# Two transformer layers on one core: the first norm taken by rows of tokens as x is loaded, and the feed-forward run on unnormed activations

## What is computed

```
def rms_norm(x, w):
    y = x * rsqrt(mean(x * x, axis=-1) + EPS)
    return y * w

# first layer
h = rms_norm(x, norm1_w)
u = h @ w_in                     # split into rnn_x, rnn_gate, q, k, v, iq, ik, iw, g
...                              # recurrent branch, indexed sparse attention, gates
x = x + merged @ w_out
h2 = rms_norm(x, norm2_w)
x = x + square(relu(h2 @ w_ff_in)) @ w_ff_out      # hidden width 4096

# second layer
u = rms_norm(x, norm1_g)
...                              # differential attention, Hyena mixer
x = x + expert_choice_ffn(rms_norm(x, norm2_g), ...)   # 16 experts, 201 MB of weights
```

## Time and profile before

| | |
|---|---|
| median of 3 runs | 1281.13 us (1275.34 to 1282.58) |
| profiled execution, its own time | 1277.17 us |
| its span | 1275.4 us |
| mean granted TensorE clock | 0.968 of full |
| PE busy | 1145.8 us (90%) |
| DVE / ACT busy | 506.4 us (40%) / 400.8 us (31%) |
| transfers | 309.32 MB, mean 243 GB/s |

### The profile page before, as it was taken

How to read it: one execution, slowest core, us unless ns; L and a number is a source line. 1 busy time by engine, 2 the same in 40 slices (tenths; PEclk the granted TensorE clock), 3 DMA queues, 4 the chain that set the end, 5 groups by cost and what they waited for, 6 DMA issues and landing times.

```text
span 1275.4 us, 16258 instructions
## 1 busy us (share of the span) xinstructions
PE 1145.8 (90%) x6528; PEld 802.6 (63%) x6528; DVE 506.4 (40%) x969; ACT 400.8 (31%) x768; POOL 16.3 (1%) x28
## 2 busy tenths in 40 slices
PE   5999998999989999989899999698897888789886
PEld 4788887877889999989577888333232323233231
DVE  2356666478376755567867532300100010001001
ACT  2241555664466644466244520200000000000000
POOL 3000000000000000000000000000000000000000
PEclk9899999989989999999999999799998999999999
DMA  6153333143235666635123195399999999999997
GB/s 215 67 207 132 133 132 133 66 149 133 94 113 190 197 175 173 180 133 198 66 77 122 67 383 211 132 393 428 428 429 429 428 429 429 429 429 428 428 425 295
DMA packets 93900, 309.32 MB, mean 243 GB/s; under 512 B 5968, under 2 KB 38872, under 8 KB 81880
## 3 DMA queue, kind: packets, MB, share of 16 engines
q1 hardware_dynamic: 93256, 307.49, 62.4%
q0 software_dynamic: 496, 1.07, 0.4%
q10 hardware_dynamic: 96, 0.02, 0.0%
HBM read 307.53 MB, written 1.05 MB: 242 GB/s over the span
## 4 chain that ended last, share of the span: by engine, by line
PE 65%; DMA 26%; DVE 5%; ACT 2%; issue 1%; SPq 0%; DVEq 0%; ACTq 0%
PE bank L422 64%; DMA arena<-in_w_up 16%; DMA arena<-in_w_down 9%; DVE rstd L1501 2%; DVE parts L1535 1%; DMA cst<-table 1%; ACT parts L1169 0%; ACT root L1123 0%; PE bank L522 0%; PE bank L618 0%; SPq L1062 0%; DVE xh L1510 0%; DVE arena L1650 0%; DVE arena L1805 0%; DVE arena L1808 0%
## 5 line engine op out<-in xcount | busy, mean ns | idle before, releaser
L422 PE MATMUL bank<-parts 128*128 128x256 f32 (+1 forms) x2640 | 341.3, 291 | 8.4 <-DVE parts L1549 8.1
L422 PEld LDWEIGHTS bank<-parts 128*128 128x128 f32 x2640 | 328.7, 194 | 24.5 <-issue 20.7
L422 PE MATMUL bank<-arena 128*32 128x512 f32 (+6 forms) x724 | 267.8, 537 | 18.3 <-DVE arena L1650 5.7
L1535 DVE TENSOR_TENSOR parts<-ring,parts 128x512 fp32r<-128x512 f32 x288 | 193.1, 689 | 122.0 <-ACT parts L1169 120.7
L1169 ACT ACTIVATE parts<-ring 128x512 fp32r<-128x512 f32 x288 | 178.1, 628 | 185.7 <-PE bank L422 184.4
L422 PE MATMUL bank<-parts_room,arena 128*32 128x512 f32 x384 | 166.9, 628 | 20.5 <-DMA arena<-in_w_up 11.2
L422 PEld LDWEIGHTS bank<-arena 128*32 128x32 f32 (+3 forms) x724 | 103.8, 173 | 51.4 <-issue 35.1
L2001 DVE TENSOR_TENSOR arena<-bank,arena 128x512 f32<-128x512 f32 x8 | 5.1, 685 | 278.0 <-ACT arena L1444 278.0
L422 PE MATMUL bank<-cst,arena 128*32 128x512 f32 (+2 forms) x226 | 98.1, 589 | 17.5 <-DMA arena<-in_w_gate 8.2
L422 PE MATMUL bank<-xh,arena 128*32 128x512 f32 (+1 forms) x224 | 94.1, 596 | 16.4 <-DMA parts_room<-in_w_up 8.2
L422 PE MATMUL bank<-hidden_parts,parts 128*128 128x256 f32 x768 | 92.3, 283 | 0.0
(11 more groups left out here) (249 smaller groups left out, 828.7 us busy)
## 6 DMA issues: line engine op xcount, KB each, us to landing
ring<-in_w_in SPq DMA_DIRECT2D x22, 2048.0 KB, 7.9
ring<-in_w_gate SPq DMA_DIRECT2D x16, 2048.0 KB, 27.1
parts_room<-in_w_up SPq DMA_DIRECT2D x16, 2048.0 KB, 27.1
ring<-in_w_ff_in SPq DMA_DIRECT2D x8, 2048.0 KB, 8.6
ring<-in_w_ff_out SPq DMA_DIRECT2D x8, 2048.0 KB, 9.0
cst<-in_w_gate SPq DMA_DIRECT2D x8, 2048.0 KB, 24.0
arena<-in_w_gate SPq DMA_DIRECT2D x8, 2048.0 KB, 28.5
xh<-in_w_up SPq DMA_DIRECT2D x8, 2048.0 KB, 25.6
```

What stands on the lines that cost most here:

```text
L422: return nc.tensor.matmul(o, lhsT=l, rhs=r, start=first, stop=last)
L1535: X.tensor_tensor(w_part[1][:, p % PIECES], piece_of(n, p), w_part[0][:, p % PIECES].bitcast(F32), ALU.subtract).then_inc(S("pieces split" ...
```

## The change

At the start, the sums of squares are taken while tokens still lie over partitions: ACT squares the first 128 tokens and DVE the last 128, with a running sum, then one root and one reciprocal of 128 x 2. Each half is scaled by its row factor and PE turns the scaled rows as well (16 more transposes, into banks 0 to 3); DVE and ACT write `hT` from there, times `norm1`. `squares(0)`, `norm_stats(0)` and `norm(0, "norm1")` are gone. x is loaded in two halves, unit 0 is issued right behind them, the identity and the row of `norm1` go by ACT's queue, and the rest of the table and of the vectors follow unit 0.

In the feed-forward, ACT rounds `xT` times `norm2` into `ff_part` without the token factor, block by block as blocks become final, and DVE takes the rests. relu(r a) squared is r squared times relu(a) squared, so r squared, 1 / (mean + EPS), is multiplied in by DVE on each tile of `w_ff_out` before it is added. The mean still comes from 8 float32 matmuls of PE, now between the two halves of the feed-forward.

```
+            pe.wait_ge(S("identity loaded"), 16)
+            pe.wait_ge(S("norm loaded"), 16)
+            ps = take(0, "norm")
+            nc.tensor.transpose(ps[:, 0:KD], vrows[0:KD, 0, :], ident[0:KD, 0:KD]).then_inc(S("norm turned"), 1)
+            for t in range(TT):
+                pe.wait_ge(S(f"x {t} loaded"), 16)
...
+            for b in range(4):
+                ps = take(b, ("h", b))
+                for t in range(TT):
+                    if b == 0:
+                        pe.wait_ge(S(f"x {t} scaled"), 1)
+                    for k in (2 * b, 2 * b + 1):
+                        c = (k % 2) * T + t * P
+                        last = nc.tensor.transpose(ps[:, c:c + P], xnormed[:, t, k * P:k * P + P], ident)
+                last.then_inc(S("h turned"), 1)
...
-            norm_stats(1)
             ub = at["ff in"] = list(use)
...
+            norm_stats(1, xsq2, "squares of x", [1 + k // 4 for k in range(KD)])
...
+            A(xsquared[:, 0, :], xtok[:, 0, :], ACT.Square, accum_out=xsq[:, 0:1]).then_inc(S("x squares"), 1)
+            act.wait_ge(S("x squares"), 1)
+            act.wait_ge(S("x squares by vector"), 1)
+            A(xroot, xsq, ACT.Sqrt, scale=1.0 / D, bias=eps).then_inc(S("x root"), 1)
+            act.wait_ge(S("x scale"), 1)
+            A(xnormed[:, 0, :], xtok[:, 0, :], ACT.Copy, scale=xscale[:, 0:1]).then_inc(S("x 0 scaled"), 1)
...
-            squares(1, lambda: round_next(PIECES, FF_IN, FF_PIECES))
-            root_of(("stats", 1), T, "norm stats", 2)
-            round_h(hT, "normed", [KD + k + 1 for k in range(KD)])
+            def round_x(k):
+                wait_taken((16 + k // 4, (k // 2) % 2))
+                A(ff_part[0][:, k, :], xT[:, k, :], ACT.Copy, scale=V("norm2", k)).then_inc(S("h rounded"), 1)
+
+            for k in range(KD - 2):
+                round_x(k)
+            round_next(PIECES - 1, FF_IN, FF_PIECES)
+            round_x(KD - 2)
+            round_x(KD - 1)
+            round_piece(0, PIECES - 1, FF_IN, FF_PIECES)
...
+            for h in range(2):
+                A(xsq2[:, 4 * h:4 * h + 4, :], xT[:, 4 * h:4 * h + 4, :], ACT.Square).then_inc(S("squares of x"), 1)
...
+            dve.wait_ge(S("norm stats"), 1)
+            empty(X.tensor_scalar(root[:, 0:T], ps(("stats", 1))[:, 0:T], EPS, None, ALU.add), ("stats", 1))
+            wait_taken(("stats", 1))
+            link(X.reciprocal(rstd[:, 0:T], root[:, 0:T]))
...
-                X.tensor_tensor(xk, bank[c][:, 0:T].unsqueeze(1), xk, ALU.add).then_inc(emptied[c], 1)
+                X.tensor_tensor(sqr[:, c, 0:T], bank[c][:, 0:T], rstd[:, 0:T], ALU.mult).then_inc(S("hidden scaled"), 1)
+                dve.wait_ge(S("hidden scaled"), i * 2 + (c + 1))
+                X.tensor_tensor(xk, sqr[:, c, 0:T].unsqueeze(1), xk, ALU.add).then_inc(emptied[c], 1)
```

More of the change, by code:

```diff
@@ L730, in _ @@
                 use[b] += 4
-            norm_stats(2)
+            norm_stats(2, hT, "squares", [k + 1 for k in range(KD)])
             for n in range(L2, L2 + 3):
@@ L1093, in ps @@
                 return bank[bank_of[job][0]]
-            for name, src in vec_loads[0][1::2]:
+            act.dma_start(cst[:, 0:P], table[:, 0:P]).then_inc(S("identity loaded"), 16)
+            act.dma_start(vrows[0:KD, 0, :], vec_loads[0][0][1]).then_inc(S("norm loaded"), 16)
+            for name, src in vec_loads[0][2::2]:
                 load_rows(act, name, src)
+            act.wait_ge(S("constants set"), 1)
+            A(xroot[:, 0:1], eps, ACT.Sqrt).then_inc(S("first root"), 1)
+            act.wait_ge(S("x 0 loaded"), 16)
+            A(xsquared[:, 0, :], xtok[:, 0, :], ACT.Square, accum_out=xsq[:, 0:1]).then_inc(S("x squares"), 1)
[4 more added lines that the diff above has]
+            A(xnormed[:, 0, :], xtok[:, 0, :], ACT.Copy, scale=xscale[:, 0:1]).then_inc(S("x 0 scaled"), 1)
+            wait_taken("norm")
+            for b in (0, 2):
+                act.wait_ge(S("h turned"), b + 1)
+                for i in range(2):
+                    k = 2 * b + i
+                    ins = A(hT[:, k, :], bank[b][:, i * T:i * T + T], ACT.Copy, scale=V("norm1", k))
+                empty(ins, ("h", b))
             for b in (1, 3):
@@ L1184, in round_h @@
                     A(h_part[0][:, k, :], src[:, k, :], ACT.Copy).then_inc(S("h rounded"), 1)
-            act.wait_ge(S("lambda ready"), 1)
-            A(lw[1], lw[1], ACT.Exp).then_inc(S("lambda exp"), 1)
-            squares(0)
-            root_of(("stats", 0), T, "norm stats", 1)
             hidden_sine(0)
@@ L1200, in _ @@
             hidden_sine(2)
-            round_h(hT, "normed", [k + 1 for k in range(KD)])
+            for b in range(4):
+                wait_taken(("h", b))
+            for k in range(KD):
+                A(h_part[0][:, k, :], hT[:, k, :], ACT.Copy).then_inc(S("h rounded"), 1)
             act.wait_ge(S("pads set"), 1)
@@ L1334, in _ @@
                 round_piece(3, p, FF_OUT, FF_PIECES + FF_IN_PIECES)
-            squares(2, lambda: round_half(LATE + 8))
-            root_of(("stats", 2), T, "norm stats", 3)
-            round_h(hT, "normed", [2 * KD + k + 1 for k in range(KD)])
+            squares(lambda: round_half(LATE + 8))
+            root_of(("stats", 2), T, "norm stats", 2)
+            round_h(hT, "normed", [k + 1 for k in range(KD)])
             def hy_half(j):
```

107 lines of the change are left out of this document (67 added, 40 removed).

## The result

The changed kernel takes **1267.67 us** (median of 4 runs, 1263.03 to 1270.57), the kernel before on the same chip 1281.86 (4 runs, 1275.34 to 1285.09): a ratio of 0.9885, 95% interval 0.9861 to 0.9909. The profiled execution took 1268.03 us, 9.1 less than that of before (1277.17); the spans, 1275.4 and 1266.2, differ by 9.2. The gain is there and lies in both places named, but the start gave 6.7 us where the forecast had 9.8.

What follows compares the result with a forecast made beforehand. A chain of PE work ahead of the expert weight stream was taken to bound the kernel; 9.8 + 6.0 - 0.5 = 15.3 us gave 1261.9 from the profiled execution, 1265.8 from the median; middle 1264, range 1257 to 1273.

Steps and rivals of the forecast that it cites:

- the first term: At the start: the first projection begins at 14.0 us, full clock, and the start gains 9.8 us (bounds 7 and 11.5).
- Scaling 1024 elements: At the start: ACT 1.14 us, DVE 0.8, done at 9.8, hidden 0.4 ahead of the first transposes' end at 10.2.
- nine slow and seven fast: At the start: of the 16 other transposes, nine take 0.23 us and seven 0.11, done at 13.1.
- So the row moves when x is through: At the start: the norm row on ACT's queue lands about 6.5 us, before the first transpose; taken between 5.8 and 8.0.
- rival (d): At the start: norm row lands only with unit 0's end, 12.5 us; 6 less, 9.3 gained, 1270; chance 0.10.
- microsecond to spare: At the start: unit 0, the first projection's weights, lands at 12.8 us, one microsecond before it is needed.
- Rival (c): At the start: transposes do not hold the clock, first projection slow; 13.0 us gained, 1266; chance 0.05.
- Rival (b): Clock falls anyway at the first projection (1.5 us) and the feed-forward's first bank (3); 10.8 gained, 1268.5; chance 0.15.
- The feed-forward, 6.0: Second term: first feed-forward bank 9.7 us sooner, less 3.6 to 3.8 for statistics between the halves; 6.0 us gained.
- The two squares: In the feed-forward: two ACT squares of 128 x 1024, 2.2 us, fit into a bank; without that room 2 us lost.
- The third term: Behind the feed-forward: the eighth tile's product with r squared lies in the chain before the last norm; 0.5 us lost.
- Rival (e): At the experts: the gain is lost in the expert weight stream, whose queue is full for 412 us; 1280; chance 0.05.

Runs made afterwards that it cites:

- the start alone: The changed kernel with the feed-forward's norm put back as before; 1275.1 us (6 runs), ratio 0.9932 to the kernel before.
- the three timed versions: The changed kernel with GpSimd's padded-key memsets behind the transposes (1265.06 us), with ScalarE scaling both halves (1265.95), or with memsets and block-weight loads behind the transposes (1263.62).
- The late-row run: The changed kernel with the norm1 row loaded by SyncE's queue behind unit 0 instead of ScalarE's queue ahead of x; 1273.55 us, one run.
- the memsets late: The changed kernel with GpSimd's two memsets of the padded keys moved behind the transposes; 1265.06 us (4 runs), ratio 0.9858 to the kernel before.
- the feed-forward alone: The changed kernel with the start put back as before; 1276.72 us (11 runs), ratio 0.9953 to the kernel before.
- the repeat: The changed kernel run again unaltered for a second trace; 1267.69 us (4 runs) against 1284.1 for the kernel before, ratio 0.9876.

## Why the prediction came out as it did

**The whole.** 1264 was forecast and 1267.7 measured, inside 1257 to 1273. The sum for the profiled execution said 1261.9; it was 1268.0. Of the 6.1, 3.1 are the first term, 3.1 the clock between the second projection and the feed-forward, 0.1 the feed-forward, and 0.2 come back behind it. The medians' difference, 14.2, lies near the forecast's 15.3, and that is partly luck: the terms as measured in the chain add up to 12.3 (below).

**The first term, 9.8, was mis-sized.** It measured 6.74 in this pair of profiles (against the other trace of the old start, 33.80, it would be 8.6). The mechanism was right: no statistics, transposes straight behind the landing, a first projection at full clock in eleven of twelve executions. The step that failed is "Scaling 1024 elements: ACT 1.14 us, DVE 277 and 354 ns for 128 and 256, so 0.8; done at 9.8". ACT took 1.15; DVE took 4.00, because GpSimd's memsets, which had stood beside nothing urgent, now stood beside a `tensor_scalar`. I had priced the instruction from rows in which POOL was idle (and rightly: 0.75 with POOL idle) and not looked at what POOL does from 8 to 12 us in the new order. The prediction itself had the warning: "covered, but barely; each microsecond over it counts fully". Its end slipped from 9.4 (8.6 + 0.8) by forecast to 12.21, a wait of 1.86 on PE. Of the second 16 transposes I had nine slow and seven fast, 2.9 us; all were slow, 3.88 in two pieces. That second part came with the first, but one execution with the wait had part of them fast (14 in 2.33 us, the start alone), so the wait alone does not settle it. The rest is small: 0.4 back because they began at 9.77 and not at 10.2, 0.4 more behind the last transpose (1.27 for 0.9) and 0.3 more around the transposes of the vectors. Where no such wait stood between, all 16 took 1.91, 2.86 and 2.89 us in the three timed versions, and those versions gained 9.3 to 9.7 (31.95 less 22.67, 22.38 and 22.22): the forecast's 9.8, nearly.

**Two steps were wrong without harm.** "So the row moves when x is through and lands about 6.5": it was there at 5.09. Its queue moved 115 packets in 2 to 4 us of the changed kernel, beside x, so x alone does not explain the stillness in the earlier trace rows, and what does stays open. The late-row run shows what the row costs if it is late: 3.8 us for a landing at 13.3, where rival (d) had 6. And unit 0 had no "microsecond to spare": with the memsets late, the first projection waited until 14.23 for it. In the changed kernel the scaling hid that. The Trainium skill, DMA: Bandwidth & Descriptors, section Queues, rings and completion order, has the DMA engines take queues in turn; the 115 packets beside x agree with it, and it leaves the 3 us without a packet in the kernel before unexplained. SyncE's queue and ACT's in 2 to 4 us of the changed kernel:

```profile
q1 hardware_dynamic: 128, 0.50, 65.0%
q10 hardware_dynamic: 115, 0.05, 13.3%
```

**Rival (c), by the rule that transposes do not count for the clock, is refuted here.** In the run with late memsets all of the second 16 ran at 273 ns with only transposes before them; in the other versions without warming and without a wait a part of them did (2.24 to 2.89 us for 16), and the first projection ran at full rate in all of these. It does not always come so soon: in the trace of the feed-forward alone the statistics behind the 16 transposes were still slow for the most part, 5.59 us in place of 3.7. The rule is that of the Trainium skill, TensorE: Matmul & The Clock Gate, Part 4 (PE-mode transpose); for float32 transposes of this size the measurement decides against it.

**Rival (b) exists and was rare:** one of twelve executions at the start, none of twelve at the feed-forward.

**The feed-forward, 6.0, measured 5.87.** The parts too: 9.3 us at the first bank (368.06 - 355.08 = 12.98, less the 3.67 by which the mixer ended earlier), forecast 9.7; the statistics 3.61 (priced at 3.4 to 3.6 by leaving seven out); the wait in the first pieces 0.5, forecast 0.8. The two squares ran as forecast in 1.99 us under a bank, whose period stayed 5.76 (418.44 to 424.20 on ACT). **The third term,** 0.5, measured 0.45 where it arises: from the start of the last norm's statistics to PE's next matmul it was 7.49 us before (545.88 to 553.37) and is 7.94 now (536.34 to 544.28). The 0.3 over the whole rest can't be held against it: the changed kernel's second trace has 732.8 us there for 729.9. **Rival (e)** fell: the stream from 843 us is at 425 GB/s and as long as before.

**Where the medians stand.** The profile's difference is 9.2 us, the medians' 14.2, and 16.4 in the later comparison. The execution of before that was profiled had little low clock for its kernel: 1277.2 at a mean of 0.968, where the 17 runs of the first comparison have a median of 1283.3 at 0.957 to 0.966. The mean clock is not all of it, for single runs at 0.965 and 0.966 took 1273.55 to 1285.33 us. And its start was the cheaper of the two that were traced, by 1.85 us. The chain's own terms in this pair, 6.74 + 5.87 - 0.3 = 12.3, lie inside the interval of the first comparison (11.7 to 17.8 us from 0.9861 and 0.9909 of 1281.86), but just outside that of the repeat (12.7 to 19.1 from 0.9851 and 0.9901 of 1284.1). With the other old start they would be 14.2. What the change is worth is somewhere from 12 to 16 us; the traces don't settle it closer.

## What to carry to other kernels

When a change moves work to an idle stretch of VectorE, read GpSimd's rows of that stretch as well: an idle-looking memset of 1.8 us cost 3 us on the path through an instruction that it shared nothing with in the program. Price an instruction under the neighbours that it will have, not those that it had; here ScalarE, `tensor_tensor` or a later memset each gave back 2.5 to 3.5 us at the second projection. Look at what stands ahead of a helper instruction in every engine's list: the five matmuls that were to warm PE held up the scale by 0.86 us. And before a few microseconds between two profiles are given a cause, multiply length by granted clock in a stretch that wasn't changed.

## What the runs showed of the hardware

- VectorE's `tensor_scalar` of 128x1024 float32 took 0.75 us with GpSimd idle, 1.01 to 1.25 beside its issuing of transfers, 2.66 to 4.21 with a 128x2048 memset near it; `tensor_tensor` of the same size 1.23 with those memsets right behind it, ScalarE's activation 1.13 in the middle of one.
- `tensor_scalar` and copies that read a PSUM bank weren't held by the same memsets: 1.75 us for four of 128x256 and 1.28 for two of 128x512, with and without them.
- The one from SBUF was held although the memset's record began 1.2 to 1.4 us after its own. The Trainium skill's page SBUF - State Buffer gives the ports to whoever issues first; by these records VectorE was first and was held all the same. The record of a memset may begin late; no run here settles it.
- Float32 transposes run at 0.23 us apiece (421 ns each) at the start and at 0.11 (273 ns) behind others, all 16 or a part of them, with nothing but transposes ahead; matmuls of zeros ahead of them shortened the first 16 from 3.64 to 2.65 us.
- One and the same kernel spent 322.2 and 318.8 us on the same 1753 matmuls in two executions, at 0.96 and 0.97 of the clock. The old start had its second projection at 31.95 in one execution and at 33.80 in another.
